# State-space step widths computed inside the projection stage instead of in a stage of their own

## The chip, the cores and the metric

The kernel runs on one core of a Trainium2 chip. The metric is the device time of one execution in microseconds (us); the median of three executions of the kernel before is 5344.7 us (5342.57 to 5345.53).

## The reference

Two transformer blocks over 512 latent and 256 context tokens of width 1024. The change touches the first block alone, where the token mixer has a state-space branch. From the normalised and modulated tokens h it takes a projection of 3072 columns, a centred convolution of three taps over the tokens and a silu, and, for 2 directions x 32 heads = 64 columns, the step widths dt and their log decays la:

```python
p_lat = h_lat @ w_in
p_ctx = h_ctx @ w_in
...
xbc = jax.nn.silu(dwconv_centred(xbc_raw, conv_w, conv_b))
...
dt = jax.nn.softplus(dt_raw.astype(jnp.float32).reshape(Bsz, L, 2, SSD_HEADS)
                     + dt_bias.astype(jnp.float32))
la = dt * (-jnp.exp(a_log.astype(jnp.float32)))
```

Both are inputs of the state-space scan that follows. Everything is float32.

## The kernel before

The program is a list of stages (`block1`), each a class with one method for each engine: `sync` (SyncE, which issues the weight loads), `tensor`, `scalar`, `vector`, `gpsimd`. Between two stages every compute engine drains and waits for the other three (L3723 to L3727), so no compute of one stage runs beside compute of another. Only SyncE runs ahead: its loads go into two weight slots that take turns over all stages (`Weights`), each load waiting until TensorE has used what was in its slot (L362).

The stages that matter here, in order: `Modulation` and `Norm` (which write h), `Xbc`, `Dt`, `SsdStates`.

`Xbc` computes the 3072 projected columns as 24 tiles of 128, feature-major: TensorE multiplies a tile's 8 weight blocks (128x128, stationary) with the 512 latent and then the 256 context tokens (L709, L710, both through the helper at L386), ScalarE copies the sums out of PSUM into a padded row (L726, L727), VectorE convolves (`conv3`, L679 to L683), ScalarE applies the silu (L733, L734). Two PSUM sets and two row buffers take turns, so TensorE's tile j waits for ScalarE's copy of tile j-2 and ScalarE's copy of tile j for VectorE's convolution of tile j-2. Beside that runs a guest, `SideModulation`: in each tile VectorE reduces one 512 KB block (L598, L605) that GpSimd has loaded (L588), with condition rows that GpSimd loads at the start of the stage (L555) and ScalarE passes through a silu (L559). Before TensorE's first tile stands a wait for `copied` (L707), which ScalarE raises by 2 behind the issue of that silu (L719, L720).

`Dt` is a stage of its own behind it. TensorE computes 128 tokens x 64 columns six times (NT = 6 token blocks), each as 8 products whose stationary operand is a 128x128 block of tokens and whose moving operand is 64 weight columns (L774). Then VectorE adds the bias (L789), ScalarE takes abs and exp (L781, L783), and VectorE evaluates log(1 + exp(-|x|)) as a series (L793 to L809) and multiplies with the decay (L812), each instruction on 128x384 elements and behind a drain.

`SsdStates` begins with two memsets on VectorE (L913); a meeting of all engines opens each of its ten passes (`meet`, L819 to L822). In a pass ScalarE copies twelve blocks (L870), TensorE sums decays (L895, L896), ScalarE takes their exp (L872), TensorE transposes 20 blocks (L901), VectorE weights them (L919, L923), ScalarE copies out (L874) and TensorE multiplies (L907).

Of the kernel before, what the change touches and what calls it, by code (L numbers as in the profile page):

```python
# [20 lines left out]
P = 128  # L21
D = 1024
KD = D // P
# [662 lines left out]
class Xbc(Stage):  # L686


    def __init__(self, chip, side):
        super().__init__(chip)  # L690
        self.side = side
        self.w = Weights(chip, "w_xbc", KX, D)
        self.h_lat, self.h_ctx = chip.view(A_HL, KD, TL), chip.view(A_HC, KD, TC)
# [5 lines left out]

    def sync(self, sp):  # L700
        self.w.load(sp)

    def tensor(self, pe):
        for i in range(0, KX // 2):
            for u in range(2):
                self.w.landed(pe, i, u)
# [10 lines left out]
    def scalar(self, act):  # L717
        a = self.nc.scalar
        self.side.silu(act, 0)  # L719
        act.sem_inc(self.copied, 2)  # L720
        act.wait_ge(self.padded, 1)
        for i in range(0, KX // 2):
            for u in range(2):
                self.w.summed(act, i, u)
                act.wait_ge(self.convolved, 2 * i + u + 1)
                a.activation(self.raw[u][:, PL:PL + TL], self.chip.bank(2 * u, TL), ACT.Copy)  # L726
                a.activation(self.raw[u][:, PC:PC + TC], self.chip.bank(2 * u + 1, TC), ACT.Copy  # L727
                             ).then_inc(self.copied, 1)
# [23 lines left out]


class Dt(Stage):


    def __init__(self, chip):
        super().__init__(chip)
        self.w = Weights(chip, "w_dt", 1, KD * 64)
        self.h_lat, self.h_ctx = chip.view(A_HL, KD, TL), chip.view(A_HC, KD, TC)  # L760
        self.dt, self.la = chip.view(DT, NT * 64), chip.view(LA, NT * 64)
        self.y, self.s, self.s2, self.q = (chip.view(SSDW + n * NT * 64, NT * 64) for n in range(4))
        self.decay = chip.view(SSDW + 4 * NT * 64, 64)
        self.steps = [chip.sem(f"dt_{s}") for s in ("biased", "exp", "decay")]

    def sync(self, sp):
        self.w.load(sp)

    def tensor(self, pe):
        self.w.landed(pe, 0, 0)  # L770
        w = self.w.view(0, KD, 64)
        for t in range(NT):
            h, at = (self.h_ctx, t * P) if t < 2 else (self.h_lat, (t - 2) * P)
            last = products(self.nc, self.chip.bank(0, 64, 64 * t), [(h[:, k, at:at + P], w[:, k]) for k in range(KD)])  # L774
        last.then_inc(self.w.used(0), 1)

    def scalar(self, act):
        biased, expd, decay = self.steps
        self.nc.scalar.activation(self.decay, self.chip.vec("a_log"), ACT.Exp).then_inc(decay, 1)
        act.wait_ge(biased, 1)  # L780
        self.nc.scalar.activation(self.y, self.dt, ACT.Abs)  # L781
        act.drain()
        self.nc.scalar.activation(self.y, self.y, ACT.Exp, scale=-1.0).then_inc(expd, 1)  # L783

    def vector(self, dve):
        v = self.nc.vector
        biased, expd, decay = self.steps
        self.w.summed(dve, 0, 0)
        v.tensor_tensor(self.dt.rearrange("p (t h) -> p t h", h=64), self.chip.bank(0, NT * 64).rearrange("p (t h) -> p t h", h=64),  # L789
                        across(self.chip.vec("dt_bias"), NT), ALU.add).then_inc(biased, 1)  # L790
        dve.wait_ge(expd, 1)

        v.tensor_scalar(self.s, self.y, 2.0, None, ALU.add)  # L793
        dve.drain()
        v.reciprocal(self.s, self.s)
        dve.drain()
        v.tensor_tensor(self.s, self.s, self.y, ALU.mult)
        dve.drain()
        v.tensor_tensor(self.s2, self.s, self.s, ALU.mult)
        dve.drain()  # L800
# [2985 lines left out]
```

## Time and profile before

| | us |
|---|---|
| median of 3 executions | 5344.7 |
| the profiled execution, its device time | 5339.45 |
| its span in the profile | 5337.7 |
| TensorE busy (share of the span) | 4669.9 (87%) |
| VectorE busy | 2669.5 (50%) |
| ScalarE busy | 1226.5 (23%) |
| GpSimd busy | 759.9 (14%) |

The span is what the profiler recorded on the core from first to last instruction; the device time holds 1.75 us around it. The shares are averages over all stages, which have different limits, so they say little of one stage. What a stage costs is read from the times at which its first and last instructions start.

### The profile page before, as it was taken

Reading aid. Unit: us, or ns where it says so; the run is one execution under the profiler, and the core shown is the slowest. Engines: PE = TensorE matmul, PEld = TensorE weight load, DVE = VectorE, ACT = ScalarE, POOL = GpSimd, SP = SyncE. Lnnn points to the kernel's source line nnn. Section 1 sums busy time; section 2 is a strip of 40 time slices with the busy share of each in tenths; the row PEclk is TensorE's granted clock in tenths of the full one; section 3 lists DMA queues with packets and bytes.
Section 4 is the critical chain, followed back from the end, with each engine's and each line's share of the span. In section 5 each row is a group of like instructions: output and inputs, shape, how many; then the busy total and the mean of one; then the engine's idle time right before and its main releaser. Section 6 shows DMA issues by size and latency. Waiting matters only on the chain.

```text
span 5337.7 us, 72125 instructions
## 1 busy us (share of the span) xinstructions
PE 4669.9 (87%) x28910; PEld 2981.7 (56%) x28910; DVE 2669.5 (50%) x4577; ACT 1226.5 (23%) x2249; POOL 759.9 (14%) x942
## 2 busy tenths in 40 slices
PE   6987797989989989998979843799887999999998
PEld 3555744544578534555545522799744555456687
DVE  2447853631388321577566487355533444423465
ACT  2112412430021010111010164222212444301230
POOL 0004410000000000111000056656100000000000
PEclk8989998989999989999989966899998999999999
DMA  3312141012112211344112255344211111021222
GB/s 144 103 57 87 56 153 66 32 64 95 62 66 85 81 53 40 129 156 169 40 47 97 90 186 208 104 111 110 80 44 48 36 36 36 12 95 67 70 84 79
DMA packets 152502, 451.24 MB, mean 85 GB/s; under 512 B 73200, under 2 KB 73456, under 8 KB 130800
## 3 DMA queue, kind: packets, MB, share of 16 engines
q1 hardware_dynamic: 128464, 350.91, 19.5%
q0 software_dynamic: 22848, 92.29, 5.0%
q8 instruction: 231, 3.78, 0.3%
q10 hardware_dynamic: 864, 3.47, 0.2%
q14 instruction: 95, 0.78, 0.1%
HBM read 377.42 MB, written 69.21 MB: 84 GB/s over the span
## 4 chain that ended last, share of the span: by engine, by line
PE 62%; issue 9%; DVE 9%; POOLq 7%; PEld 4%; ACT 2%; DMA 2%; DVEq 2%; POOL 1%; PEldq 0%; ACTq 0%; SPq 0%
PE psum L386 53%; PEld psum L386 4%; POOLq L2828 3%; POOLq L2826 3%; PE psum L648 1%; DVE sbuf L1091 1%; PE psum L2386 1%; DVE sbuf L663 1%; PE psum L2387 1%; PE psum L2358 1%; DVE sbuf L2533 1%; PE psum L1029 1%; DVE sbuf L666 1%; PE psum L1244 1%; DVE sbuf L1100 1%
## 5 line engine op out<-in xcount | busy, mean ns | idle before, releaser
L386 PE MATMUL psum<-sbuf 128*128 128x512 f32 (+3 forms) x10256 | 3316.5, 483 | 204.2 <-DVE sbuf L1592 52.0
L386 PEld LDWEIGHTS psum<-sbuf 128*128 128x128 f32 (+1 forms) x10256 | 1938.5, 192 | 1539.1 <-issue 1205.6
L3428 PE MATMUL psum<-sbuf 64*64 64x64 f32 (+1 forms) x10752 | 423.7, 237 | 23.5 <-SPq L3337 14.0
L3428 PEld LDWEIGHTS psum<-sbuf 64*64 64x64 f32 x10752 | 410.0, 138 | 39.9 <-SPq L3337 15.5
L598 DVE CUSTOM_DVE_ANT_0 sbuf<-sbuf 128x1024 f32<-128x1024 f32 x160 | 212.9, 1331 | 42.2 <-DMA sbuf<-w_side 26.7
L1604 DVE SCALAR_TENSOR_TENSOR sbuf<-psum,sbuf 128x256 f32<-128x256 f32 (+2 forms) x288 | 125.8, 480 | 193.2 <-PE psum L386 188.6
L3023 PE MATMUL psum<-sbuf 64*128 64x512 f32 (+2 forms) x192 | 87.7, 728 | 143.8 <-POOL sbuf L2985 65.1
L3553 ACT ACTIVATE sbuf<-psum 128x256 f32<-128x256 f32 (+3 forms) x384 | 128.5, 368 | 359.2 <-PE psum L3428 293.6
L631 ACT ACTIVATE sbuf<-sbuf 128x512 f32<-128x512 f32 (+1 forms) x114 | 52.9, 552 | 620.0 <-DVEq L3727 602.9
L588 POOL DMA_DIRECT2D sbuf<-w_side x128 | 68.4, 535 | 858.7 <-DVE sbuf L598 858.0
L3023 PEld LDWEIGHTS psum<-sbuf 64*128 64x128 f32 (+1 forms) x192 | 40.7, 270 | 186.6 <-POOL sbuf L2985 70.9
L2827 POOL TENSOR_TENSOR sbuf<-sbuf 96x30 f32<-96x30 f32 (+14 forms) x240 | 135.4, 564 | 52.3 <-issue 19.4
L1861 DVE TENSOR_TENSOR sbuf<-sbuf 128x512 f32<-128x512 f32 x40 | 27.8, 694 | 228.1 <-ACT sbuf L1851 228.1
L555 POOL DMA_DIRECT2D sbuf<-cond_rows x4 | 2.4, 604 | 946.9 <-DVEq L3727 863.7
L2825 POOL TENSOR_TENSOR sbuf<-sbuf 96x30 f32<-96x30 f32 (+14 forms) x240 | 129.6, 540 | 33.7 <-issue 1.7
L1467 DVE TENSOR_TENSOR sbuf<-sbuf,psum 128x512 f32<-128x512 f32 x16 | 10.3, 685 | 240.6 <-PE psum L386 240.6
L3658 DVE TENSOR_SCALAR sbuf<-psum,sbuf 128x64 f32<-128x64 f32 x192 | 45.9, 280 | 149.6 <-PE psum L3428 148.0
L648 PE MATMUL psum<-sbuf 128*128 128x512 f32 (+1 forms) x228 | 93.8, 570 | 29.8 <-ACT sbuf L631 29.8
L2533 DVE TENSOR_REDUCE sbuf<-psum 128x1 f32<-128x768 f32 x64 | 61.2, 956 | 108.2 <-PE psum L2387 108.2
L2484 POOL TENSOR_TENSOR sbuf<-sbuf 64x512 f32<-64x512 f32 x16 | 20.3, 1269 | 664.6 <-ACT sbuf L2419 433.7
L1592 DVE TENSOR_TENSOR sbuf<-sbuf 128x1024 f32<-128x1024 f32 (+1 forms) x100 | 100.0, 1004 | 29.3 <-DMA sbuf<-w_sgu_out 9.6
L679 DVE TENSOR_SCALAR sbuf<-sbuf 128x512 f32<-128x512 f32 (+1 forms) x68 | 36.2, 533 | 155.4 <-ACT sbuf L727 153.0
(310 smaller groups left out, 5156.9 us busy)
## 6 DMA issues: line engine op xcount, KB each, us to landing
sbuf<-w_side POOLq DMA_DIRECT2D x128, 512.0 KB, 3.9
sbuf<-w_sgu_uz SPq DMA_DIRECT2D x32, 1088.0 KB, 5.1
sbuf<-terms SPq DMA_DIRECT2D x115, 256.0 KB, 2.8
sbuf<-w_up SPq DMA_DIRECT2D x22, 1024.0 KB, 4.9
sbuf<-w_merge SPq DMA_DIRECT2D x8, 2560.0 KB, 9.1
sbuf<-w_mla_head SPq DMA_DIRECT2D x16, 1152.0 KB, 5.1
sbuf<-w_sgu_v SPq DMA_DIRECT2D x8, 2048.0 KB, 7.9
sbuf<-w_sgu_out SPq DMA_DIRECT2D x8, 2048.0 KB, 8.2
```

The costliest lines, as they stand in the source:

```text
L386: last = nc.tensor.matmul(out, w, x, start=(n == 0), stop=(n == len(pairs) - 1))
L598: last = v.tensor_tensor_reduce(junk, self.slot[b], self.rows[:, c], 1.0, 0.0, ALU.mult, ALU.add, self.sums[:, b, n:n + 1])
L648: last = self.nc.tensor.matmul(self.chip.bank(n, t), self.chip.const("ones"), squares[:, i], start=(i == 0), stop=(i == k - 1))
L1604: last = v.scalar_tensor_tensor(x[:, m], self.chip.bank(i)[:, cols], gates[sign][:, m:m + 1], x[:, m], ALU.mult, ALU.add)
L2533: v.tensor_reduce(self.mx[:, n:n + 1], self.s_bank(n), AX.X, ALU.max)
L2825: engine.tensor_tensor(product, left, right, ALU.mult)
L2826: eng.drain()
L2827: engine.tensor_tensor(x[:, j + 1:BLK, 0:j], x[:, j + 1:BLK, 0:j], product, ALU.add)
L2828: eng.drain()
L3023: last = t.matmul(out[:, at:at + width], w, x[:, at:at + width], start=True, stop=True)
L3428: last = t.matmul(out[hs], lhs[hs], rhs[hs], start=start, stop=stop)
L3553: copy = lambda to, of: a.activation(to, of, ACT.Copy)
```

## The change

The stage `Dt` goes; its work moves into `Xbc`.

- TensorE computes the step widths before the first tile of the projection, feature-major: 64 weight columns are stationary and all tokens move. The 8 weight blocks are split in two halves of 4, whose sums go to the partitions 0 to 63 and 64 to 127 of the PSUM banks 4 and 5 (`dt_products`).
- ScalarE copies both halves out (`dt_raw`, 128x768), TensorE turns them back to token-major with 6 transposes between tile 0 and tile 1 (`dt_turns`), and VectorE adds bias and both halves behind tile 0's convolution and reduction (`dt_sums`).
- ScalarE takes abs and exp before its copy of tile 2. VectorE runs the series behind tile 3's convolution and reduction (`dt_steps`).
- `w_dt` is loaded first, and so every tile of `w_xbc` lies in the other weight slot than before. The first two weight loads no longer are the first two tiles of `w_xbc`: tile 1 now waits until `w_dt` has been used.

```diff
@@ -689,7 +689,16 @@
     def __init__(self, chip, side):
         super().__init__(chip)
         self.side = side
+        self.w_dt = Weights(chip, "w_dt", 1, KD * 64)
         self.w = Weights(chip, "w_xbc", KX, D)
+        self.dt, self.la = chip.view(DT, NT * 64), chip.view(LA, NT * 64)
+        at = A_W + D
+        self.dt_raw = chip.view(at, T)
+        self.dt_y, self.dt_s, self.dt_s2, self.dt_q = (chip.view(at + T + n * NT * 64, NT * 64) for n in range(4))
+        self.dt_decay = chip.view(at + T + 4 * NT * 64, 64)
+        assert D + T + 4 * NT * 64 + 64 <= WSLOT
+        self.dt_raw_out, self.dt_turned, self.dt_biased, self.dt_exp, self.dt_decay_out = (
+            chip.sem("dt_" + n) for n in "raw_out turned biased exp decay".split())
         self.h_lat, self.h_ctx = chip.view(A_HL, KD, TL), chip.view(A_HC, KD, TC)
         self.xbc = chip.view(XBC, KX, T)
         self.raw = [chip.view(SSDW + u * PAD, PAD) for u in range(2)]
@@ -697,12 +706,75 @@
         self.padded, self.copied, self.convolved, self.activated = (
             chip.sem("xbc_" + s) for s in ("padded", "copied", "convolved", "activated"))
 
+    def dt_wide(self):
+        return self.chip.psum[:, 4:6].rearrange("p b w -> p (b w)")
     def sync(self, sp):
+        self.w_dt.load(sp)
         self.w.load(sp)
 
+    def dt_products(self, pe):
+        self.w_dt.landed(pe, 0, 0)
+        w = self.w_dt.view(0, KD, 64)
+        for k in range(KD // 2):
+            for at, h, n in ((0, self.h_lat, TL), (TL, self.h_ctx, TC)):
+                for half in range(2):
+                    last = self.nc.tensor.matmul(self.dt_wide()[64 * half:64 * half + 64, at:at + n], w[:, KD // 2 * half + k],
+                                                 h[:, KD // 2 * half + k], start=(k == 0), stop=(k == KD // 2 - 1))
+        last.then_inc(self.w_dt.used(0), 1)
+    def dt_turns(self, pe):
+        pe.wait_ge(self.dt_raw_out, 1)
+        for t in range(NT):
+            last = self.nc.tensor.transpose(self.dt_wide()[:, P * t:P * t + P], self.dt_raw[:, P * t:P * t + P], self.chip.const("ident"))
+        last.then_inc(self.dt_turned, 1)
+    def dt_sums(self, dve):
+        v = self.nc.vector
+        dve.wait_ge(self.dt_turned, 1)
+        for first, to, n in ((0, 2, NT - 2), (NT - 2, 0, 2)):
+            out = self.dt.rearrange("p (t h) -> p t h", h=64)[:, to:to + n]
+            halves = self.dt_wide()[:, P * first:P * first + P * n].rearrange("p (t a h) -> p t a h", a=2, h=64)
+            v.tensor_tensor(out, halves[:, :, 0], across(self.chip.vec("dt_bias"), n), ALU.add)
+            dve.drain()
+            last = v.tensor_tensor(out, out, halves[:, :, 1], ALU.add)
+        last.then_inc(self.dt_biased, 1)
+    def dt_steps(self, dve):
+        v = self.nc.vector
+        dve.wait_ge(self.dt_exp, 1)
+        y, s, s2, q, dt = self.dt_y, self.dt_s, self.dt_s2, self.dt_q, self.dt
+        v.tensor_scalar(s, y, 2.0, None, ALU.add)
+        dve.drain()
+        v.reciprocal(s, s)
+        dve.drain()
+        v.tensor_tensor(s, s, y, ALU.mult)
+        dve.drain()
+        v.tensor_tensor(s2, s, s, ALU.mult)
+        dve.drain()
+        v.tensor_scalar(q, s2, 1.0 / 17, None, ALU.mult)
+        for n in (15, 13, 11, 9, 7, 5, 3):
+            dve.drain()
+            v.scalar_tensor_tensor(q, q, 1.0 / n, s2, ALU.add, ALU.mult)
+        dve.drain()
+        v.scalar_tensor_tensor(q, q, 1.0, s, ALU.add, ALU.mult)
+        v.tensor_scalar(dt, dt, 0.0, None, ALU.max)
+        dve.drain()
+        v.scalar_tensor_tensor(dt, q, 2.0, dt, ALU.mult, ALU.add)
+        dve.wait_ge(self.dt_decay_out, 1)
+        dve.drain()
+        v.scalar_tensor_tensor(self.la.rearrange("p (t h) -> p t h", h=64), dt.rearrange("p (t h) -> p t h", h=64),
+                               -1.0, across(self.dt_decay, NT), ALU.mult, ALU.mult)
     def tensor(self, pe):
+        self.dt_products(pe)
         for i in range(0, KX // 2):
             for u in range(2):
+                if (i, u) == (0, 1):
+                    self.dt_turns(pe)
                 self.w.landed(pe, i, u)
                 pe.wait_ge(self.copied, 2 * i + u + 1)
                 w = self.w.view(u, KD, P)
@@ -718,9 +790,17 @@
         a = self.nc.scalar
         self.side.silu(act, 0)
         act.sem_inc(self.copied, 2)
+        a.activation(self.dt_decay, self.chip.vec("a_log"), ACT.Exp).then_inc(self.dt_decay_out, 1)
+        self.w_dt.summed(act, 0, 0)
+        a.activation(self.dt_raw, self.dt_wide()[:, 0:T], ACT.Copy).then_inc(self.dt_raw_out, 1)
         act.wait_ge(self.padded, 1)
         for i in range(0, KX // 2):
             for u in range(2):
+                if (i, u) == (1, 0):
+                    act.wait_ge(self.dt_biased, 1)
+                    a.activation(self.dt_y, self.dt, ACT.Abs)
+                    act.drain()
+                    a.activation(self.dt_y, self.dt_y, ACT.Exp, scale=-1.0).then_inc(self.dt_exp, 1)
                 self.w.summed(act, i, u)
                 act.wait_ge(self.convolved, 2 * i + u + 1)
                 a.activation(self.raw[u][:, PL:PL + TL], self.chip.bank(2 * u, TL), ACT.Copy)
@@ -749,68 +829,10 @@
                 conv3(self.nc, dve, self.acc[u][:, 0:T + 1], self.raw[u],
                       [self.chip.vec_at("conv_w", k * KX + j) for k in range(3)], T + 1).then_inc(self.convolved, 1)
                 self.side.reduce(dve, 0, i, u)
-class Dt(Stage):
...
+                if (i, u) == (0, 0):
+                    self.dt_sums(dve)
+                if (i, u) == (1, 1):
+                    self.dt_steps(dve)
 
 
 SPARE = [A_W + u * WSLOT + D for u in range(2)]
@@ -1791,7 +1813,7 @@
         Inputs(chip),
         Modulation(chip, "w_mod1", 4, ("c", "c_ctx"), "b_mod", A_MOD1),
         Norm(chip, "norm_in", [job_lat, job_ctx], A_WORK),
-        Xbc(chip, side), Dt(chip), SsdStates(chip), SsdOutput(chip),
+        Xbc(chip, side), SsdStates(chip), SsdOutput(chip),
         GateZ(chip, side),
         (load := LoadContext(chip)),
         Norm(chip, "norm_ssd", [dict(x=y, out=y, gain=chip.vec("ssd_g"))], SSDW),
```

On TensorE, between the sums of the stage `Norm` (L648) and the second tile of the projection (L386), before:

```order
L648 MATMUL psum<-sbuf 128x256 x8
L386 MATMUL psum<-sbuf 128x512 x8
L386 MATMUL psum<-sbuf 128x256 x8
L386 MATMUL psum<-sbuf 128x512 x8
L386 MATMUL psum<-sbuf 128x256 x8
```

and after the change, where L723 is `dt_products` and L730 `dt_turns`:

```order
L648 MATMUL psum<-sbuf 128x256 x8
L723 MATMUL psum<-sbuf 64x512 x2
L723 MATMUL psum<-sbuf 64x256 x2
L723 MATMUL psum<-sbuf 64x512 x2
L723 MATMUL psum<-sbuf 64x256 x2
L723 MATMUL psum<-sbuf 64x512 x2
L723 MATMUL psum<-sbuf 64x256 x2
L723 MATMUL psum<-sbuf 64x512 x2
L723 MATMUL psum<-sbuf 64x256 x2
L386 MATMUL psum<-sbuf 128x512 x8
L386 MATMUL psum<-sbuf 128x256 x8
L730 MATMUL psum<-sbuf 128x128 x6
```

16 products and 6 transposes have come in; the 48 products of 64 columns that stood behind the 24th tile (L774 through L386) are gone.

On VectorE, behind the reduction of tile 3 (L598, L605), after the change; the rows L750 to L769 are `dt_steps`, which before stood, with the same shapes, behind the last tile of the stage:

```order
L605 TENSOR_TENSOR sbuf<-sbuf 128x1
L750 TENSOR_SCALAR sbuf<-sbuf 128x384
L752 RECIPROCAL sbuf<-sbuf 128x384
L754 TENSOR_TENSOR sbuf<-sbuf 128x384
L756 TENSOR_TENSOR sbuf<-sbuf 128x384
L758 TENSOR_SCALAR sbuf<-sbuf 128x384
L761 SCALAR_TENSOR_TENSOR sbuf<-sbuf 128x384 x7
L763 SCALAR_TENSOR_TENSOR sbuf<-sbuf 128x384
L764 TENSOR_SCALAR sbuf<-sbuf 128x384
L766 SCALAR_TENSOR_TENSOR sbuf<-sbuf 128x384
L769 SCALAR_TENSOR_TENSOR sbuf<-sbuf 128x384
L679 TENSOR_SCALAR sbuf<-sbuf 128x769
```

The convolution of tile 4 (L679) now stands behind them on the engine.

On ScalarE, from the last silu of the projection into the first pass of `SsdStates` (L870 to L874, now L892 to L896), before:

```order
L734 ACTIVATE sbuf<-sbuf 128x256
L779 ACT_TABLE_LOAD
L779 ACTIVATE sbuf<-sbuf 128x64
L781 ACTIVATE sbuf<-sbuf 128x384
L783 ACTIVATE sbuf<-sbuf 128x384
L870 ACTIVATE sbuf<-sbuf 128x1536
L872 ACTIVATE sbuf<-psum 128x64
```

and after the change:

```order
L814 ACTIVATE sbuf<-sbuf 128x256
L892 ACTIVATE sbuf<-sbuf 128x1536
L894 ACT_TABLE_LOAD
L894 ACTIVATE sbuf<-psum 128x64
```

The table for exp is now loaded inside the first pass of `SsdStates`; inside the projection ScalarE loads a table four times more (at L793, L803 and twice at L813).

## Rows read from the trace of the kernel before

**Rows 1.** Windows: length, PE, PEld, DVE, ACT, POOL busy (x), PEclk, DMA share, GB/s.

```profile
82.90:346.20 263.30, 250.03 (x768) 145.72 (x768) 100.15 (x146) 50.34 (x98) 13.35 (x25) 0.97 0.31 99
346.20:380.90 34.70, 20.74 (x96) 20.56 (x96) 10.81 (x17) 2.59 (x4) 0.00 (x0) 0.50 0.00 1
```

**Rows 2.** Timeline across Dt: start, length, engine, line, idle before.

```profile
345.95 0.16 DVE L605 TENSOR_TENSOR sbuf<-sbuf 128x1 f32<-128x1 f32 x1
...
346.25 20.74 PE L386 MATMUL psum<-sbuf 128*128 128x64 f32 x96 [5.57 <-DVEq L3727]
...
368.77 0.36 DVE L793 TENSOR_SCALAR sbuf<-sbuf 128x384 f32<-128x384 f32 x1 [1.19 <-ACT sbuf L783]
...
379.89 0.56 DVE L812 SCALAR_TENSOR_TENSOR sbuf<-sbuf 128x384 f32<-128x384 f32 x1
381.10 1.76 DVE L913 MEMSET sbuf<- 128x2048 f32 x1 [0.64 <-DVEq L3727]
```

**Rows 3.** Timeline at the start of the projection.

```profile
82.76 1.28 ACT L559 ACT_TABLE_LOAD   x1
...
90.48 2.76 ACT L559 ACTIVATE sbuf<-sbuf 128x3072 f32<-128x3072 f32 x1 [6.44 <-DMA sbuf<-cond_rows]
...
90.65 59.90 PE L386 MATMUL psum<-sbuf 128*128 128x512 f32 x175 [19.63 <-ACTq L720]
...
102.80 0.60 ACT L726 ACTIVATE sbuf<-psum 128x512 f32<-128x512 f32 x1 [9.55 <-PE psum L386]
...
113.09 0.60 ACT L726 ACTIVATE sbuf<-psum 128x512 f32<-128x512 f32 x1 [9.42 <-PE psum L386]
```

**Rows 4.** Windows: clock at the projection's start.

```profile
92.00:94.00 2.00, 2.00 (x4) 0.76 (x3) 0.00 (x0) 1.25 (x1) 0.00 (x0) 0.59 0.04 16
94.00:96.00 2.00, 2.00 (x6) 0.87 (x5) 0.00 (x0) 0.00 (x0) 0.00 (x0) 1.00 0.00 0
```

**Rows 5.** Attention stage, column halves (128*64): its line, and a window of it.

```profile
L1294 PEld LDWEIGHTS psum<-sbuf x288: 132/134/232, 919.5 to 1141.6; 128*64 128x64 f32 x144
...
919.48:921.36 1.88, 1.88 (x16) 1.04 (x16) 1.00 0.00 0
```

**Rows 6.** Timeline, fifth tile and last tile of the projection.

```profile
144.13 0.60 ACT L726 ACTIVATE sbuf<-psum 128x512 f32<-128x512 f32 x1 [5.48 <-PE psum L386]
...
145.04 0.62 DVE L679 TENSOR_SCALAR sbuf<-sbuf 128x769 f32<-128x769 f32 x1 [5.87 <-ACT sbuf L727]
...
149.37 0.16 DVE L605 TENSOR_TENSOR sbuf<-sbuf 128x1 f32<-128x1 f32 x1
...
340.72 0.60 ACT L726 ACTIVATE sbuf<-psum 128x512 f32<-128x512 f32 x1 [9.47 <-PE psum L386]
```

**Rows 7.** Timeline, first pass of SsdStates and one transpose row of the second.

```profile
385.06 1.50 ACT L870 ACTIVATE sbuf<-sbuf 128x1536 f32<-128x1536 f32 x1 [16.32 <-DVEq L821]
...
385.96 4.51 PE L901 MATMUL psum<-sbuf 128*128 128x128 f32 x20
386.46 0.21 ACT L872 ACTIVATE sbuf<-psum 128x64 f32<-128x64 f32 x1
386.70 0.19 DVE L919 TENSOR_TENSOR sbuf<-sbuf 128x32 f32<-128x32 f32 x1 [0.89 <-ACT sbuf L872]
...
389.65 0.69 DVE L923 TENSOR_TENSOR sbuf<-psum,sbuf 128x512 f32<-128x512 f32 x1 [0.16 <-PE psum L901]
390.51 0.60 ACT L874 ACTIVATE sbuf<-psum 128x512 f32<-128x512 f32 x1 [3.83 <-PE psum L901]
...
391.16 3.71 PE L907 MATMUL psum<-sbuf 128*128 128x512 f32 x8 [0.69 <-ACT sbuf L874]
...
396.54 2.41 PE L901 MATMUL psum<-sbuf 128*128 128x128 f32 x20
```

**Rows 8.** Loads: SyncE's issues up to 110 us, and w_xbc to landing.

```profile
45.36 57.86 SPq L363 DMA_DIRECT2D sbuf<-w_xbc  x3
...
DMA to landing us min/median/max: 3.3/3.5/4.5
```

More of the change, by code:

```diff
@@ L751, in vector @@
                 self.side.reduce(dve, 0, i, u)
-class Dt(Stage):
[L757 to L800, printed above, removed]
-        v.tensor_scalar(self.q, self.s2, 1.0 / 17, None, ALU.mult)
-        for n in (15, 13, 11, 9, 7, 5, 3):
-            dve.drain()
-            v.scalar_tensor_tensor(self.q, self.q, 1.0 / n, self.s2, ALU.add, ALU.mult)
-        dve.drain()
-        v.scalar_tensor_tensor(self.q, self.q, 1.0, self.s, ALU.add, ALU.mult)
-        v.tensor_scalar(self.dt, self.dt, 0.0, None, ALU.max)
-        dve.drain()
-        v.scalar_tensor_tensor(self.dt, self.q, 2.0, self.dt, ALU.mult, ALU.add)
-        dve.wait_ge(decay, 1)
-        dve.drain()
-        v.scalar_tensor_tensor(self.la.rearrange("p (t h) -> p t h", h=64), self.dt.rearrange("p (t h) -> p t h", h=64),
-                               -1.0, across(self.decay, NT), ALU.mult, ALU.mult)
```

## The prediction

> **What bounds the kernel now.** The page says that TensorE is busy for 87% of the span, but that is a mean over stages that are kept apart by barriers. I therefore read the windows by stage first, then the timeline at both ends of the stages that the change touches, then single lines for the prices of what is new.
>
> The windows [rows 1] show two stages of opposite kinds. In the projection (82.9 to 346.2) TensorE is busy 250.0 of 263.3 us at a granted clock of 0.97. In `Dt` (346.2 to 380.9) it is busy 20.7 us at a clock of 0.50, which is 1.2 GHz, and VectorE 10.8 us behind that; ScalarE has 2.6 us, GpSimd nothing, and the DMA share is 0.00. The timeline [rows 2] shows them one after the other: 96 TensorE instructions for 20.74 us, then the series of VectorE from 368.77 to 380.45. Nothing runs beside it, so all of the stage is on the path.
>
> The projection has room for both. Its own pace is TensorE's: the copies of tiles 1 and 23 start at 113.09 and 340.72 [rows 3, 6], 22 tiles apart, so 10.35 us a tile. TensorE idles for 19.63 us before its first product at 90.65 and is released by ScalarE's queue [rows 3], which waits until 90.48 for the condition rows. VectorE idles 5.87 us before each convolution and has work from 145.04 to 149.53 in the tile that is shown [rows 6], so 4.5 us of 10.35.
>
> **The change, part by part.**
>
> *The stage that goes.* The last reduction of the projection ends at 346.11, the last instruction of `Dt` at 380.45, and the first memset of `SsdStates` starts at 381.10, 0.65 behind it [rows 2]. Without `Dt` the memset comes 0.65 behind 346.11, at 346.76. That is 34.34 us less. One barrier is in this number.
>
> *The products of the step widths, new ahead of tile 0.* They need h, thus the start of the stage. ScalarE's first instruction of it is at 82.76 [rows 3], and in `Dt` TensorE started 0.14 behind the last work of the stage ahead [rows 2]; I take 82.9. There are 8 products of 512 and 8 of 256 columns, the same columns as one tile of the projection: 10.35 us if they ran one by one. But neighbours go to different column halves of the array. The nearest row is the attention stage, where pairs of products of 256 columns alternate between column halves: 16 instructions in 1.88 us at full clock, 0.1175 each [rows 5] (a float32 product shows as two instructions). At one by one the same would be 10.35 / 6144 x 256 / 2 = 0.216. So the halves overlap, and the 16 instructions of 256 columns and 16 of 512 cost 1.88 + 3.76 = 5.64 us at full clock.
>
> The clock is low when they begin. At tile 0 it rose about 3.0 us after TensorE's start (mean 0.59 over 92 to 94, 1.00 behind it [rows 4]); in the first pass of `SsdStates` all 20 transposes took 4.51 us, against 2.41 in the second, so there it was low for at least 5.4 us [rows 7]. I take 4, which does 2 us of work, and 3.64 remain: the end is 82.9 + 4 + 3.64 = 90.5. With 3.0 and 5.4 it is 90.0 and 91.2. The release of tile 0 stays at 90.65. The products are hidden to within 0.6 us; I take 0. If the cover were gone (the condition rows already there at 82.9) they would cost all of their 7.6 us.
>
> A rule speaks against this. The Trainium skill, page "TensorE: Matmul & The Clock Gate", Part 3 (Packing small matmuls), says that a weight load overlaps with running products only if it goes to another row group; column halves share all rows. By that rule the sum would be that of the first rival below, 4.2 us more. The trace does not agree: 16 loads, median 0.134 us, and 16 products fit into 1.88 us [rows 5].
>
> *Tile 0.* It took 90.65 to 102.80, 12.15 us, 1.80 more than the pace, because it began at the low clock [rows 3, 4]. Now TensorE has worked up to it, and I take the clock as risen: 1.80 less. The bounds are 0 and 1.80.
>
> *The 6 transposes ahead of tile 1.* At 2.41 / 20 = 0.12 us each [rows 7] they put 0.72 us on TensorE, which paces the stage; at the low clock 1.35. They wait for ScalarE's copy of the sums: silu until 93.24, a table load of 1.28, an exp on 64 columns (0.21 in rows 7) and a copy of 768 columns (0.60 for 512, so under 1.2) end before 96, and tile 0 ends at about 101. No wait.
>
> *VectorE.* Behind tile 0 stand four additions of at most 256 columns, under 0.69 us each (the row of 512), so under 2.8 in an idle time of 5.87. Behind tile 3 stands the series: 368.77 to 380.45 is 11.68 us [rows 2]. Before the change tile 3's work on VectorE ends 5.87 ahead of 145.04, at 139.2; with the series it ends at 150.9, and the convolution of tile 4 is 5.8 late. Its work then ends at 149.53 + 5.8 = 155.3, and tile 5's is due at 145.04 + 10.35 = 155.4: made up for within one tile. What waits for the late convolution? ScalarE's copy of tile 6, due near 165, and its silu of tile 4, which stands in its queue behind the copy of tile 5 (154.5) anyway, when the convolution, begun at 150.9 and some 2.9 long, is done. TensorE waits for neither. Cost 0.
>
> *ScalarE.* Abs, a table load and exp ahead of the copy of tile 2 are 0.6 + 1.28 + 0.6 at most, in an idle time of 5.5 as in front of every even tile [rows 6]; the silu tables load in front of silus that have 9.5 us of idle time around them. Cost 0. The table load that matters stands in the first pass of `SsdStates`: exp there would end at 386.56 + 1.28 + 0.21 = 388.05 instead of 386.67. The four weightings then run back to back at 0.69 and end at about 391.05, the first at 389.0. TensorE's products started at 391.16, released by ScalarE's copy out of the transposes [rows 7], and need one weighting each. So the load hides behind transposes at the low clock; its price is 1.28 if these were fast, and then they would give back 2.1. I take 0. TensorE's pause ahead of that pass is now about 10 us (tile 23's end to the memset, 346.76 - 340.7, and 3.96 from memset to pass). A pause of 5.57 was enough for the low clock of `Dt` [rows 1, 2], so it is low again.
>
> *Loads.* The first load of `w_xbc` went out at 45.36 and the third behind tile 0's products [rows 8]. Tile 1's now goes out when the products of the step widths end, near 90.6, and lands 3.3 to 4.5 us later [rows 8], beside one more pair of side loads; it is needed at about 101.7. Cost 0, with 6 us to spare.
>
> **The sum.** -34.34 + 0.72 - 1.80 = -35.4 us. The profiled execution took 5339.45 us, so its like would take 5304.0. The median of the runs shown lies 5.25 above the profiled execution, and I keep that distance: 5344.7 - 35.4 = 5309.3 us.
>
> **The rivals.**
>
> 1. *The products of the step widths do not overlap*, either because the halves take turns (10.35) or because each of 32 weight loads stands between them (5.64 + 32 x 0.134 = 9.9). The end is 82.9 + 4 + 8.35 = 95.25, tile 0 is 4.6 late: 5313.9 us (by the loads alone 94.8, 5313.5). Against it: rows 5. For it: there the products have 256 columns, not 512. Chance 0.15.
> 2. *The clock does not rise under half-width products.* They take 11.3 us, until 94.2, 3.5 late, and tile 0 still pays its 1.80: 5314.6 us. For it: no row shows a rise under column halves alone. Chance 0.12; both rivals together (20.7 us, 13.0 late) give 5324, chance 0.03.
> 3. *The series reaches TensorE.* If the 5.8 us by which the convolution is late came through to ScalarE's copies: 5315.1 us. Against it: the queue orders above. Chance 0.05.
> 4. *The gain is given back later*, by something that `Dt` hid. In [rows 1] there is no DMA beside it and the other engines idle, so it would have to be code loading or the clock in later stages. With half given back: 5327. Chance 0.04, of which 0.02 for three quarters or more.
> 5. *Slower than before: VectorE never catches up.* If its work per tile behind the series exceeded TensorE's pace, it would pace the 20 tiles that are left. From 35.4 / 20 = 1.77 us a tile on, thus 12.1 us of VectorE work instead of 4.5, the change loses; at 12.5 us a tile the time is 5309.3 + 43 = 5352. Against it: the idle time of 5.87 in each tile [rows 6]. Chance 0.01.
>
> **How the numbers follow.** My forecast has 0.60, with a range of its own of 5305 to 5312 (0.6 for the products, up to 1.3 for the table, 1.8 for the clock at tile 0, 2.1 given back in `SsdStates`, and the 3 us by which executions of the kernel differ). The range reaches up over rivals 1 to 3, 5304 to 5316. A difference of 0.2%, 10.7 us, is about what a measurement of this kernel tells from none. Only rivals 4 and 5 come near it: faster 0.97, within 0.2% 0.02, slower 0.01.
>
> **What the profile of the changed kernel would show.** The products at L723 start near 82.9 and end near 90.5, and the first product of tile 0 still waits for ScalarE's queue, at 90.65; if it starts with no idle time ahead of it and near 94 or 95, rival 1 or 2 holds, and the clock between 86 and 94 says which. Tile 0's copy comes near 101.0, the transposes at L730 take 0.7 us, the convolution of tile 4 is the only one that is late, and the copies keep 10.35 us of distance through tiles 4 to 6. The first memset of `SsdStates` is near 345.7. Behind it every stage should look as before, only 35 us earlier. The prediction is wrong if the memset is there and the span is not 35 us shorter, or if the copies of tiles 5 to 7 spread.

## The result, and the profile after

The changed kernel takes 5306.7 us (median of 4, 5301.3 to 5306.85) against 5345.1 before: ratio 0.9922, 95% interval 0.9909 to 0.9935. It is faster, by 38 us by the medians and by 35 to 49 us by the interval. The forecast was 5309.3, which is a ratio of 0.9933 to 5345.1. The median lies in the stated range; 0.9922 x 5345.1 = 5303.4 lies 0.6 under its lower end.

The page of the changed kernel begins like this:

```profile
span 5299.5 us, 72020 instructions
## 1 busy us (share of the span) xinstructions
PE 4655.1 (88%) x28852; PEld 2961.9 (56%) x28852; DVE 2666.6 (50%) x4580; ACT 1233.2 (23%) x2254; POOL 765.7 (14%) x942
```

The span is 38.2 us shorter than 5337.7. To see how much of that the change explains, I split both spans at the first memset of the states stage, which stands behind all that was moved; of what the change touches only the table load of exp comes later. Before, it starts at 381.10 [rows 2]. After, the timeline shows:

```profile
344.96 0.16 DVE L605 TENSOR_TENSOR sbuf<-sbuf 128x1 f32<-128x1 f32 x1
345.77 1.76 DVE L935 MEMSET sbuf<- 128x2048 f32 x1 [0.65 <-DVEq L3749]
...
349.73 1.50 ACT L892 ACTIVATE sbuf<-sbuf 128x1536 f32<-128x1536 f32 x1 [5.13 <-DVEq L843]
...
350.63 4.51 PE L923 MATMUL psum<-sbuf 128*128 128x128 f32 x20
351.25 1.28 ACT L894 ACT_TABLE_LOAD   x1
352.55 0.23 ACT L894 ACTIVATE sbuf<-psum 128x64 f32<-128x64 f32 x1
352.80 0.19 DVE L941 TENSOR_TENSOR sbuf<-sbuf 128x32 f32<-128x32 f32 x1 [2.32 <-ACT sbuf L894]
...
353.07 2.48 DVE L945 TENSOR_TENSOR sbuf<-psum,sbuf 128x512 f32<-128x512 f32 x4
355.18 0.60 ACT L896 ACTIVATE sbuf<-psum 128x512 f32<-128x512 f32 x1 [2.41 <-PE psum L923]
355.83 3.71 PE L929 MATMUL psum<-sbuf 128*128 128x512 f32 x8 [0.69 <-ACT sbuf L896]
```

The head is 35.33 us shorter (381.10 - 345.77) and the tail 2.9 us (4956.6 against 4953.7). The first pass of the states stage shows the table load of exp, and shows it hidden: TensorE's products start 6.10 behind ScalarE's first instruction (349.73 to 355.83), as before (385.06 to 391.16 [rows 7]).

The second pass is not as it was. GpSimd's multiplication (L884, now L906) waits there until the store of the first pass's state has landed. First the rows before the change, then those after:

```profile
395.69 9.14 SPq L860 DMA_DIRECT2D states<-sbuf  x2
...
399.70 4.04 POOL L884 TENSOR_TENSOR sbuf<-sbuf 128x512 f32<-128x512 f32 x4 [8.85 <-ACTq L821]
```

```profile
360.36 10.72 SPq L882 DMA_DIRECT2D states<-sbuf  x2
...
365.95 4.04 POOL L906 TENSOR_TENSOR sbuf<-sbuf 128x512 f32<-128x512 f32 x4 [9.00 <-DMA states<-sbuf]
```

From the issue of the store to the multiplication pass 4.0 us before and 5.6 after. (In the first row of the multiplication the releaser named, ScalarE, was done with its exp at 397.35; the store, issued at 395.69, is the last to come.) The pass takes 8.8 us in all four profiles that still have the stage `Dt`, and 9.9 to 10.4 in eight of the nine others whose states stage is untouched. Why the store lands later is not shown. (By the code the multiplication of a pass waits for the store of the pass ahead, which is of the other direction's state, so a looser wait would do; no run tries it.) The prediction has every later stage unchanged.

At the start of the projection, the rows that answer to [rows 3] (L723 are the moved products, L730 the transposes):

```profile
82.12 7.38 PE L723 MATMUL psum<-sbuf 128*64 128x512 f32 x32 [11.74 <-ACTq L3749]
82.13 1.28 ACT L559 ACT_TABLE_LOAD   x1
...
90.32 2.76 ACT L559 ACTIVATE sbuf<-sbuf 128x3072 f32<-128x3072 f32 x1 [6.90 <-DMA sbuf<-cond_rows]
90.48 10.59 PE L386 MATMUL psum<-sbuf 128*128 128x512 f32 x32 [0.98 <-ACTq L792]
...
100.91 0.82 PE L730 MATMUL psum<-sbuf 128*128 128x128 f32 x6
101.16 0.60 ACT L806 ACTIVATE sbuf<-psum 128x512 f32<-128x512 f32 x1 [5.81 <-issue]
...
112.11 0.60 ACT L806 ACTIVATE sbuf<-psum 128x512 f32<-128x512 f32 x1 [10.08 <-PE psum L386]
```

TensorE is done with the moved products at 89.50 and still waits 0.98 us for ScalarE's queue. The windows give its clock (columns as in [rows 1]):

```profile
84.00:86.00 2.00, 2.00 (x10) 0.83 (x8) 0.00 (x1) 0.00 (x0) 1.05 (x2) 0.50 0.75 184
86.00:88.00 2.00, 2.00 (x14) 0.85 (x12) 0.00 (x0) 0.00 (x0) 0.00 (x0) 0.95 1.00 424
```

It rises at about 86.2, 4.1 us after TensorE's start, and tile 0 begins at full clock: from its start to ScalarE's copy it takes 10.68 us (90.48 to 101.16) instead of 12.15 (90.65 to 102.80 [rows 3]). VectorE in tiles 3 to 6, with the series (L750 to L769) in its new place:

```profile
138.11 0.35 DVE L750 TENSOR_SCALAR sbuf<-sbuf 128x384 f32<-128x384 f32 x1
...
148.86 0.56 DVE L769 SCALAR_TENSOR_TENSOR sbuf<-sbuf 128x384 f32<-128x384 f32 x1
149.34 0.62 DVE L679 TENSOR_SCALAR sbuf<-sbuf 128x769 f32<-128x769 f32 x1
...
153.49 0.60 ACT L806 ACTIVATE sbuf<-psum 128x512 f32<-128x512 f32 x1 [9.47 <-PE psum L386]
...
154.40 0.62 DVE L679 TENSOR_SCALAR sbuf<-sbuf 128x769 f32<-128x769 f32 x1 [0.56 <-ACT sbuf L807]
...
163.84 0.60 ACT L806 ACTIVATE sbuf<-psum 128x512 f32<-128x512 f32 x1 [5.47 <-PE psum L386]
```

One convolution is late (149.34, due near 144.05), the next one is on time with 0.56 us to spare, and ScalarE's copies keep a distance of 10.35 us.

### The profile page after: what moved, and what is told of

The parts are those of the page before. It is cut to its first block, busy times and chain, and to the rows that moved or that the text cites. A ratio compares the mean times of both kernels' runs of the same rounds, so it can differ in the third digit from the quotient of the medians.

```text
span 5299.5 us, 72020 instructions
## 1 busy us (share of the span) xinstructions
PE 4655.1 (88%) x28852; PEld 2961.9 (56%) x28852; DVE 2666.6 (50%) x4580; ACT 1233.2 (23%) x2254; POOL 765.7 (14%) x942
## 4 chain that ended last, share of the span: by engine, by line
PE 60%; issue 9%; DVE 9%; POOLq 7%; PEld 5%; DMA 3%; ACT 2%; DVEq 2%; POOL 1%; PEldq 0%; SPq 0%; ACTq 0%
PE psum L386 52%; PEld psum L386 4%; POOLq L2850 3%; POOLq L2848 3%; PE psum L648 1%; PE psum L2408 1%; DVE sbuf L663 1%; PE psum L2409 1%; DVE sbuf L1113 1%; PE psum L2380 1%; DVE sbuf L2555 1%; PE psum L1051 1%; DVE sbuf L666 1%; DMA sbuf<-w_side 1%; PE psum L1266 1%
## 5 line engine op out<-in xcount | busy, mean ns | idle before, releaser
L386 PE MATMUL psum<-sbuf 128*128 128x256 f32 (+3 forms) x10160 | 3295.7, 483 | 178.2 <-DVE sbuf L1614 51.5
L386 PEld LDWEIGHTS psum<-sbuf 128*128 128x128 f32 (+1 forms) x10160 | 1917.8, 190 | 1513.0 <-issue 1178.7
L598 DVE CUSTOM_DVE_ANT_0 sbuf<-sbuf 128x1024 f32<-128x1024 f32 x160 | 212.4, 1327 | 39.7 <-DMA sbuf<-w_side 23.1
L1883 DVE TENSOR_TENSOR sbuf<-sbuf 128x512 f32<-128x512 f32 x40 | 27.8, 694 | 228.1 <-ACT sbuf L1873 228.1
L648 PE MATMUL psum<-sbuf 128*128 128x512 f32 (+1 forms) x228 | 93.6, 569 | 29.8 <-ACT sbuf L631 29.8
L679 DVE TENSOR_SCALAR sbuf<-sbuf 128x512 f32<-128x512 f32 (+1 forms) x68 | 36.3, 533 | 142.2 <-ACT sbuf L807 140.1
```

The lines of the kernel that those rows point to most:

```text
L386: last = nc.tensor.matmul(out, w, x, start=(n == 0), stop=(n == len(pairs) - 1))
L598: last = v.tensor_tensor_reduce(junk, self.slot[b], self.rows[:, c], 1.0, 0.0, ALU.mult, ALU.add, self.sums[:, b, n:n + 1])
L648: last = self.nc.tensor.matmul(self.chip.bank(n, t), self.chip.const("ones"), squares[:, i], start=(i == 0), stop=(i == k - 1))
```

## The experiments

### Is the rest of the difference the change's?

The head explains 35.3 of 38.2 us. Both kernels were profiled again, unchanged.

> The kernel before, unchanged, profiled once more. The two profiles so far differ by 38.2 us, of which 35.3 lie between the start of the projection and the first memset of the states stage and in the stages ahead of it; the other 2.9 us come from later stages that the change does not touch (states +1.9, outputs -3.4, gate -0.7, attention -2.1, two later stages -4.2 and +4.6). Theory A (executions differ by chance): this profile differs from the first one of the same kernel by 1 to 4 us in just those stages, and the projection and the step-width stage repeat to within 0.5 us. Theory B (the change shifts them): those stages repeat to within 0.5 us here, and only the changed kernel has them otherwise.

> The changed kernel, unchanged, profiled once more. Theory A: the later stages differ from its first profile by 1 to 4 us each, the projection repeats to 0.5 us (263.1), and the three later executions of 5306.7 against 5301.3 for the profiled one are that chance. Theory B: outputs near 198.2 and attention near 297.6 again, 3.4 and 2.1 us below the kernel before. Ratio to the kernel before 0.992 to 0.9935.

Measured: 5345.4 us for the kernel before (10 executions, ratio to itself 1.0007, interval 0.9997 to 1.0017), 5307.5 us for the changed one (4 executions, ratio 0.9928, 0.9911 to 0.9944). Their spans are 5338.9 and 5314.4 us. From the timelines, first the kernel before, then the changed one:

```profile
382.27 1.76 DVE L913 MEMSET sbuf<- 128x2048 f32 x1 [0.64 <-DVEq L3727]
```

```profile
346.35 1.76 DVE L935 MEMSET sbuf<- 128x2048 f32 x1 [0.64 <-DVEq L3749]
```

The heads repeat (382.27 and 346.35, 35.9 apart). The tails do not: 4956.6 us for the kernel before, exactly as the first time, but 4968.0 for the changed one instead of 4953.7. So this time the changed kernel's tail is 11.4 us longer than before, where it was 2.9 shorter. The largest part is in one stage, the RWKV scan, which takes 525.0 and 531.1 us before and 529.7 and 539.1 after. (A stage's time is taken here and below from barrier to barrier, that is between the last drains of the four engines at its two ends.) That is theory A for the sum, and for the outputs stage too, which moved from 201.6 to 199.1 in the kernel before and from 198.2 to 199.7 in the changed one. For other stages theory B was not gone: the RWKV terms stage stood at 263.6 and 264.7 after, 267.9 and 268.2 before.

### The two halves of the theory: the gap at the start of the projection

```diff
-        self.side.silu(act, 0)
         act.sem_inc(self.copied, 2)
+        self.side.silu(act, 0)
```

> The kernel before with the signal for TensorE's first tile raised ahead of the silu of the condition rows, so that the gap of 8 us at the start of the projection closes. Theory of the forecast (that gap is what pays for the moved products): tile 0 starts near 82.9 instead of 90.65, still at the low clock, and all ends 7.8 us earlier, near 5337 us. Rival (something else holds the stage's start, a load or VectorE's reduction that needs the rows): less than 2 us.

> The same edit in the changed kernel. Theory of the forecast: TensorE is busy with the moved products until about 89.5, 1.0 us ahead of the old release, so the edit gives 1.0 us and no more (span 1 us shorter), and the difference between the two kernels with this edit is 35.3 - 7.8 + 1.0 = 28.5 us instead of 35.3. Rival (the moved products cost nothing even without the gap, or the gap is not what covers them): the difference stays near 35.

Measured: 5338.2 us for the edit in the kernel before (ratio 0.9985, 0.9974 to 0.9996), 5303.4 us in the changed one (0.9921, 0.9904 to 0.9937). The timelines, first of the edited kernel before, then of the edited changed kernel:

```profile
82.89 20.40 PE L386 MATMUL psum<-sbuf 128*128 128x512 f32 x55 [11.91 <-ACTq L719]
...
94.99 0.60 ACT L726 ACTIVATE sbuf<-psum 128x512 f32<-128x512 f32 x1 [1.42 <-PE psum L386]
```

```profile
82.99 7.20 PE L723 MATMUL psum<-sbuf 128*64 128x512 f32 x32 [11.74 <-ACTq L3749]
...
90.11 10.62 PE L386 MATMUL psum<-sbuf 128*128 128x512 f32 x32
```

In the kernel before, tile 0 starts at 82.89 and the projection stage takes 255.7 us, 8.0 less than the 263.5 and 263.8 of the unedited kernel. (In a third profile with that projection unedited, e7 below, it takes 265.1: the clock rose 6.0 us after tile 0's start instead of 3.0.) In the changed kernel tile 0 starts right behind the products, at 90.11, and the stage is 1.1 us shorter (261.9 against 263.1 and 262.9). The first memsets of the two edited kernels are 373.27 and 345.43, 27.8 us apart (28.5 expected) instead of 35.3. The gap is what pays for the moved products: whoever closes it first gets 8 us from it, and the change then is worth 27.8 by the head.

### Do the column halves overlap?

```diff
-        for k in range(KD // 2):
-            for at, h, n in ((0, self.h_lat, TL), (TL, self.h_ctx, TC)):
-                for half in range(2):
+        for half in range(2):
+            for k in range(KD // 2):
+                for at, h, n in ((0, self.h_lat, TL), (TL, self.h_ctx, TC)):
```

> The changed kernel with the products of one column half all ahead of those of the other, so that neighbours never lie in different halves. Theory of the forecast (neighbours in different halves overlap, 5.6 us at full clock against 10.35): the products take 12 us instead of 7.4, end near 94.5, tile 0 starts there with no idle time, about 4 us later than now, and the kernel is 4 us slower, near 5311. Rival (half-width products are quick by themselves): products near 7.4 us and no change.

Measured: 5306.7 us (ratio 0.9930, 0.9911 to 0.9946). The spread of executions hides 3 us, so the profile has to decide:

```profile
82.32 11.10 PE L723 MATMUL psum<-sbuf 128*64 128x512 f32 x32 [11.74 <-ACTq L3749]
...
93.35 10.62 PE L386 MATMUL psum<-sbuf 128*128 128x512 f32 x32
```

and the window of its moved products (columns as in [rows 1]):

```profile
82.32:93.35 11.03, 11.03 (x32) 4.46 (x33) 1.40 (x2) 4.40 (x3) 1.75 (x3) 0.83 0.62 238
```

The same 32 instructions take 11.10 us instead of 7.38, tile 0 starts 2.9 us later with no idle time ahead of it, and the stage takes 265.9 us instead of 263.1. With the mean clock of the window they are 11.03 x 0.83 = 9.2 us at full clock, against 7.38 x 0.72 = 5.3 in the changed kernel (0.72 is the clock of the window 82.12 to 89.50). The order of the loop is worth 2.8 us, not the 4 expected, since apart the products cost 11.1 us and not 12. That they still stay 1.2 us under the 10.35 of full width at full clock is not explained.

### Do the pauses of later tiles pay for the series?

```diff
-                if (i, u) == (1, 1):
+                if (i, u) == (KX // 2 - 1, 1):
                     self.dt_steps(dve)
```

> The changed kernel with VectorE's series behind tile 23 instead of tile 3: the same instructions with no projection tile behind them. Theory of the forecast (the pauses of later tiles pay for the series): all 11.6 us come onto the path, the projection's stage is 274.7 instead of 263.1 us and the kernel near 5318.5. Rival (the gain is from the removed stage's products and barrier, the series is cheap in any place): less than 3 us.

Measured: 5311.8 us (4 executions from 5302.5 to 5319.1; ratio 0.9932, 0.9915 to 0.9949). The timeline of its end:

```profile
345.64 0.16 DVE L605 TENSOR_TENSOR sbuf<-sbuf 128x1 f32<-128x1 f32 x1
345.71 0.35 DVE L750 TENSOR_SCALAR sbuf<-sbuf 128x384 f32<-128x384 f32 x1
...
356.45 0.56 DVE L769 SCALAR_TENSOR_TENSOR sbuf<-sbuf 128x384 f32<-128x384 f32 x1
357.66 1.76 DVE L935 MEMSET sbuf<- 128x2048 f32 x1 [0.64 <-DVEq L3749]
```

The stage takes 274.2 us, 11.0 more, and the first memset comes at 357.66. Exposed, the series costs nearly all of its length. The median rose by only 4 to 5 us of the 11 expected; with a spread of 17 us in four executions the time alone says little, and the profile carries this one.

How far does the cover reach? The series was evaluated two and three times in its place behind tile 3 (`for _ in range(2)` and `range(3)` around its steps, same values).

> The same with the series evaluated twice, 21.4 us. Theory of the forecast: the convolution of tile 5 ends near 167, the copy of tile 6 near 169.5, before TensorE wants its tile 8 at 174.2: no stall, the stage stays at 263 us. Rival (VectorE's lateness of 15.5 us reaches TensorE): 3 to 10 us.

> The changed kernel with VectorE evaluating the series three times in its place behind tile 3 (same values each time), so 31.4 us there instead of 11.4. Theory of the forecast (the late convolutions are made up for out of the pauses, 5.9 us a tile, and reach TensorE only through ScalarE's copy of tile 6): VectorE's series ends near 169.5, the convolution of tile 5 near 177, the copy of tile 6 ends near 179 instead of 165 and TensorE, due at tile 8 near 174.2, stalls about 5 us there; the stage is 268 us instead of 263 and the kernel 5 us slower. Rival (the added VectorE time comes through one for one, or is free whatever its size): 20 us, or 0.

Measured: twice 5304.9 us (ratio 0.9926, 0.9908 to 0.9944), three times 5313.9 us (0.9933, 0.9915 to 0.9951). With two evaluations the stage stays at 263.1 us; the copy of tile 6 starts at 167.48, in time. With three, the timeline shows the chain that was expected (L679 the convolutions of tiles 4 and 5, L807 and L808 the copy of tile 6):

```profile
168.22 0.62 DVE L679 TENSOR_SCALAR sbuf<-sbuf 128x769 f32<-128x769 f32 x1
...
172.67 0.62 DVE L679 TENSOR_SCALAR sbuf<-sbuf 128x769 f32<-128x769 f32 x1
...
176.54 0.57 ACT L807 ACTIVATE sbuf<-psum 128x512 f32<-128x512 f32 x1
...
177.02 0.37 ACT L808 ACTIVATE sbuf<-psum 128x256 f32<-128x256 f32 x1
...
177.53 12.73 PE L386 MATMUL psum<-sbuf 128*128 128x512 f32 x37 [2.92 <-ACT sbuf L808]
```

TensorE stalls once, at tile 8, for 2.9 us, and the stage takes 265.9 us. I had expected 5: VectorE packs the late tiles closer than their timed distance (168.22 to 172.67, 4.45 us each). Between 21 and 31 us of series in all the cover ends; the real one has 11.

### Where a stage begins, and what it calls its semaphores

Later stages might also depend on their semaphores, the counters by which the engines signal one another. An empty stage (`Stage(chip)`) in the place of the removed one gives every later stage its old semaphore numbers; one behind it in the kernel before gives them the new ones.

> The changed kernel with an empty stage where the step-width stage stood. It costs one barrier, 0.5 to 0.65 us, and gives every later stage the semaphore numbers and stage index that it has in the kernel before. Three profiles of each kernel show the RWKV terms stage at 266.7 to 268.2 before and 263.6 to 265.5 after, and attention at 298.3 to 299.6 before and 297.6 to 297.9 after, though the change does not touch them. Theory S (semaphore numbers or stage index do it): terms near 267.5 and attention near 299 again. Theory P (place of the code or time at which a stage begins does it): terms near 264.6, attention near 297.8. Theory C (chance): either, no pattern.

> The kernel before with an empty stage behind the step-width stage: 0.5 to 0.65 us more, and later stages get the semaphore numbers that they have in the changed kernel, with the code in nearly the place of before. Theory S: terms near 264.6, attention near 297.8, the whole about 3 to 4 us faster than the kernel before in spite of the barrier. Theory P: terms near 267.5, attention near 299, whole 0.6 us slower.

Measured: 5304.2 us (ratio 0.9921, 0.9905 to 0.9938) and 5342.8 us (1.0004, 0.9993 to 1.0015). The terms stage takes 265.3 us in the first and 267.6 in the second: it stays with its kernel, not with its semaphores. Theory S falls. Attention, 299.5 in the first and 299.7 in the second, fits neither theory; it is 299.2 in the profile with two evaluations of the series, which has neither an empty stage nor the old one. The barrier of an empty stage is 0.49 us.

For theory P the changed kernel got the empty stage and 29 small products on TensorE behind its last tile.

```diff
+        pe.wait_ge(self.dt_biased, 1)
+        c = self.chip.const("ident")[:, 0:32]
+        for _ in range(29):
+            self.nc.tensor.matmul(self.chip.bank(4, 32)[0:32], c, c, start=True, stop=True)
```

> The changed kernel with the empty stage and with 29 small products on TensorE (32x32, sums unused) behind its last tile of the projection, where it waits 5 us for VectorE, so that TensorE's code behind that stage starts about as far into its program as in the kernel before. Theory P (the place of TensorE's code makes the terms stage 3 us shorter): terms near 267.5 instead of 264.5. Rival (another engine's code, or something that is carried from stage to stage): terms 263.6 to 265.5 as in all six profiles of variants of the changed kernel so far. The products themselves cost at most 1 us.

Measured: 5308.9 us (ratio 0.9932, 0.9916 to 0.9948). The terms stage takes 266.7 us, between the two values, and attention 297.6. That decides nothing. Over all profiles of this study the terms stage has 266.7 to 268.2 us in four with the old stage and 263.0 to 266.7 in ten without it. Why stays open. It is not seen in the whole tail: the four tails of the kernels with the old stage are 4956.6, 4956.6, 4959.9 and 4957.4 us, mean 4957.6; the nine of the changed kernel and of its variants with an untouched tail are 4953.7, 4968.0, 4958.1, 4959.5, 4953.7, 4959.7, 4956.2, 4960.9 and 4957.6, mean 4958.6. But the scan, which alone varies by 14 us over these profiles, happens to be 3.6 us longer on average in the nine. Without it the tails, counted from the barrier ahead of the states stage, are 4420.0 to 4426.0 us in the four (mean 4423.7) and 4417.1 to 4424.1 in the nine (mean 4421.1). The 2.6 us between the means have a standard error of 1.7. They are made of terms (3.0 shorter), outputs (1.9 shorter), attention (1.1 shorter), states (2.6 longer) and 0.8 longer in the rest. So a tail that is 2 to 3 us shorter is neither shown nor excluded.

### A version that beats both

The early signal, and the memsets of the states stage moved behind the first meeting, to GpSimd, which waits there anyway:

```diff
-        for d in range(2):
-            v.memset(self.state[d], 0.0)
...
             meet(pool, self.met, n)
+            if n < 2:
+                self.nc.gpsimd.memset(self.state[d], 0.0)
+                pool.drain()
             pool.wait_ge(self.weighted, n + 1)
```

> A version meant to beat the changed kernel: the early signal for tile 0 (1.0 us), and the two memsets that open the states stage moved from VectorE ahead of the first meeting to GpSimd behind it, where GpSimd waits for ScalarE's exp. Theory (those memsets stand alone on the path, 3.96 us from the first memset to the first pass): the first pass begins 3.9 us earlier relative to the end of the projection, all 4.9 us faster than the changed kernel, near 5302. Rival (GpSimd's memset takes longer than its wait for the exp, and the first two passes stretch): 1 to 3 us, with GpSimd's multiplications later in passes 1 and 2.

Measured: 5299.1 us (median of 5, 5292.3 to 5303.7), ratio 0.9912, 0.9898 to 0.9926. Its timeline:

```profile
346.09 0.70 DVE L939 COPY sbuf<-sbuf 128x1024 f32<-128x1024 f32 x1 [0.55 <-POOLq L843]
...
346.16 2.37 POOL L903 MEMSET sbuf<- 128x2048 f32 x1 [20.75 <-POOLq L843]
...
349.21 4.04 POOL L909 TENSOR_TENSOR sbuf<-sbuf 128x512 f32<-128x512 f32 x4 [0.68 <-ACT sbuf L894]
...
356.43 1.80 POOL L903 MEMSET sbuf<- 128x2048 f32 x1 [3.17 <-DVEq L843]
356.45 2.32 DVE L939 COPY sbuf<-sbuf 128x1024 f32<-128x1024 f32 x1
```

The first pass begins 0.56 us behind the projection's last reduction (345.53 to 346.09) instead of 4.61 (345.12 to 349.73), and GpSimd's memset ends before the exp. In the second pass it does not stay free: VectorE's copy beside it takes 2.32 us instead of 0.69. That is not seen in the time of the passes, though: the first two take 20.5 us together (346.09 to 366.63), against 21.1 in the changed kernel (349.73 to 370.79), where the second one waits for the store. So the 4.05 us are kept, and about 1 comes from the signal: 5 us, as expected. The median is 7.6 to 8.5 us below the changed kernel's; the part above 5 is of the size by which the tails differ, and is not claimed.

## Why the prediction was right or wrong

- *The stage that goes, -34.34.* By the barriers of the traces it took 34.35 us in the kernel before, and the barrier behind the projection is still 0.65. Right.
- *The products, 0.* Right, and the reason too: 7.38 us against 7.6 forecast (6.88 to 7.68 in nine profiles with this order), clock rise after 4.1 us, end 0.98 us ahead of the release. The halves overlap (5.3 us at full clock, 5.64 forecast); rival 1 held 9.9 to 10.35, and apart they take 9.2. Rival 2 falls by the window's clock. The prediction left out the row that spoke most for that rival: in `Dt` the clock stood at 0.50 through all 20.7 us of products [rows 1], and that products of 64 moving columns and products of 64 stationary ones differ in this was not known from any row.
- *Tile 0, -1.80.* It gave 12.15 - 10.68 = 1.47 from start to copy. The 12.15 is no constant: in e7 the same tile of the kernel before took 13.7, by the later rise of the clock.
- *The transposes, +0.72.* The copies of tiles 0 and 1 are 10.95 us apart instead of 10.29 [rows 3]: 0.66.
- *What differs by chance.* The condition rows came later within the stage: ScalarE's silu starts 8.19 us behind its first instruction instead of 7.72 [rows 3], 0.47 us on the path. That is not the change's: the same distance is 8.01 in the second profile of the kernel before and 7.96 in that of the changed one. The stage itself is thus 0.36 us shorter in this pair of profiles, not 1.08, and what stood ahead of it happened to be 0.63 us shorter. 34.35 + 0.36 + 0.63 = 35.3, so the head of this one pair meets the forecast partly by luck. Over more profiles the sum holds: projection and `Dt` take 297.8, 298.2 and 299.4 us together in three profiles (the two of the kernel before, and e7), the projection alone 262.7 to 263.1 in five (the two of the changed kernel, e6, e10, e13). The means are 35.5 us apart, where the prediction has 34.34 + 1.08 = 35.42.
- *VectorE, ScalarE, the table load, the loads, 0 each.* Right: the copies keep their distance, the first pass of the states stage is as long as before, and TensorE waits nowhere in the projection for a load. Rival 3 needs more than 21 us of series, where there are 11; rival 5 did not come with 31 either, where TensorE stalled once.
- *The step that failed is the one for all that lies behind the change*: later stages at 0 ("every stage should look as before"), with "the 3 us by which executions of the kernel differ" as their only room in the range. Those 3 us were the spread of three executions. In the comparisons of this study the kernel before ran from 5330.4 to 5358.2 us, and the changed kernel, in eight executions, from 5301.3 to 5316.2. A ratio such as the one above is good to some 7 us, and the range of 5304 to 5316 left no room for that below. Nor do single later stages look as before: the scan alone differs by 9.5 us between two profiles of the changed kernel, and the terms, outputs and states stages have other means with and without `Dt`. By the ratio the gain is 41.7 us, 6.3 more than the sum, by the medians 38.4. Over all 55 executions of the kernel before and the eight of the changed one the means (5344.5 and 5306.8) are 37.7 us apart, with a standard error of 1.8. That agrees with 35.4, and it would also agree with a tail 2 to 3 us shorter. So the excess of the result is at least in part chance; whether the rest of it is the change's stays open.

## What to carry to other kernels

A stage between barriers whose engines take turns costs its whole length, so look for neighbours with idle time on just those engines, and price each moved piece by the pause that takes it up: here 7.4 us of TensorE in a gap of 8.4 behind a load, and 11 us of VectorE in pauses of 5.9 us a tile that add up over several tiles. Such a gap can be spent once: with the gap closed the same change is worth 7.5 us less (27.8 instead of 35.3). And where executions of one kernel differ by 25 us, split the span at the first instruction behind the change; the head repeats to about 1 us (381.10 and 382.27, 345.77 and 346.35) where the whole does not.

## What the runs showed of the hardware

- Float32 products of 64 columns in alternating column halves overlap almost fully: 7.38 us, of which 4.1 at half clock, thus 5.3 us at full clock for what takes 10.35 at full width, with 32 weight loads of 0.138 us (median) in between. In one half after the other the same products take 9.2.
- The granted clock rose 3.1 to 4.7 us after the start of products that fill only half of the columns each (nine profiles, alternating halves), and 2.9, 3.0, 3.1 and 6.0 us after the start of full-width ones (four profiles of the projection with its old start). Under the products of `Dt` it did not rise in 20.7 us.
- A memset of 2048 columns on GpSimd and a copy of 1024 columns on VectorE did not run side by side: whichever began second took longer by about what the first still had to go. The copy, begun 0.02 us behind the memset, took 2.32 us instead of 0.69; the memset, begun 0.07 us behind the copy in the pass before, took 2.37 instead of 1.80, and the copy 0.70 (two passes of one profile).
- The same program on the same chip differed by up to 25 us from execution to execution (5330.4 to 5355.3 in one comparison), and the RWKV scan alone by 9.5 us (529.7 to 539.1) between two profiles of the changed kernel.
